# Bias tables read back by one skewed DMA in their final values and ordered by copies on GpSimd, in place of matmuls on TensorE

## The reference, cut to what matters

```python
def grouped_head_bias(bias_table, dist, ...):       # rel_bias (32, 20)
    return bias_table[rel_bucket(dist)]             # one value per distance and head
# heads 0-3: dense attention, 4-11: the compressed/selected/windowed branch, 12-19: window of 128 with sinks
s = q @ k.T * scale + grouped_head_bias(...)        # masked where dist < 0 (heads 12-19 also dist >= 128)
s_c = q @ k_cmp.T * scale + bias(qpos - cmp_end)    # cmp_end = 16 b + 31, b = 0..14
```

## Time and profile before

| what | us |
|---|---|
| median of 3 runs (3497.65 to 3503.95) | 3498.44 |
| the profiled execution | 3502.94 |
| its span | 3501.2 |
| TensorE busy | 3340.7 (95%) |
| VectorE busy | 1847.7 (53%) |
| ScalarE busy | 1565.8 (45%) |
| GpSimd busy | 143.6 (4%) |

### The profile page before, as it was taken

How to read it: one execution, slowest core, us unless ns; L and a number is a source line. 1 busy time by engine, 2 the same in 40 slices (tenths; PEclk the granted TensorE clock), 3 DMA queues, 4 the chain that set the end, 5 groups by cost and what they waited for, 6 DMA issues and landing times.

```text
span 3501.2 us, 39804 instructions
## 1 busy us (share of the span) xinstructions
PE 3340.7 (95%) x16471; PEld 2776.9 (79%) x16471; DVE 1847.7 (53%) x2387; ACT 1565.8 (45%) x1918; POOL 143.6 (4%) x253
## 2 busy tenths in 40 slices
PE   8999999949999989999999999999999999999998
PEld 6898888837888878878888878886788788867886
DVE  5455455555455455454465454654554645544545
ACT  4344344424444444443344343465544534565444
POOL 0000000002000000000000000012100000122000
PEclk9999999969999999999899999999999999999999
DMA  6545555513555545555456545642455455633553
GB/s 211 191 158 180 182 186 186 170 60 97 184 180 192 180 149 176 186 176 185 147 161 202 171 158 189 186 134 97 141 187 186 162 183 178 172 100 113 187 190 109
DMA packets 323905, 576.24 MB, mean 165 GB/s; under 512 B 45258, under 2 KB 130353, under 8 KB 323597
## 3 DMA queue, kind: packets, MB, share of 16 engines
q1 hardware_dynamic: 321196, 566.71, 49.9%
q0 software_dynamic: 2384, 6.63, 0.7%
q10 hardware_dynamic: 144, 0.35, 0.0%
HBM read 571.53 MB, written 1.08 MB: 164 GB/s over the span
## 4 chain that ended last, share of the span: by engine, by line
PE 90%; DVE 5%; ACT 3%; issue 1%; DMA 0%; DVEq 0%; SPq 0%; ACTq 0%
PE up L1668 20%; PE up L1670 19%; PE up L1669 19%; PE acc L1668 8%; PE acc L1670 8%; PE acc L1669 8%; DVE w_lo L944 2%; ACT w_hi L564 2%; PE up L1943 1%; PE acc L1838 1%; PE up L2160 1%; DVE xT_lo L1056 1%; PE acc L1765 0%; ACT xT_hi L629 0%; PE acc L1845 0%
## 5 line engine op out<-in xcount | busy, mean ns | idle before, releaser
L944 DVE TENSOR_TENSOR w_lo<-raw,w_hi 128x2048 fp32r<-128x2048 f32 x543 | 1244.4, 2292 | 1352.9 <-ACT w_hi L564 1350.2
L564 ACT ACTIVATE w_hi<-raw 128x2048 fp32r<-128x2048 f32 x543 | 1040.7, 1917 | 1470.6 <-PE up L1670 1094.9
L1668 PE MATMUL up<-w_hi,xT_hi 128*128 128x512 f32 (+1 forms) x2500 | 989.8, 396 | 54.9 <-DVE xT_lo L1056 27.1
L1669 PE MATMUL up<-w_lo,xT_hi 128*128 128x512 f32 (+1 forms) x2500 | 979.1, 392 | 0.0
L1670 PE MATMUL up<-w_hi,xT_lo 128*128 128x512 f32 (+1 forms) x2500 | 979.0, 392 | 0.0
L1668 PEld LDWEIGHTS up<-w_hi,xT_hi 128*128 128x128 f32 x2500 | 474.2, 190 | 166.5 <-issue 49.5
L1670 PEld LDWEIGHTS up<-w_hi,xT_lo 128*128 128x128 f32 x2500 | 474.0, 190 | 98.6
L1669 PEld LDWEIGHTS up<-w_lo,xT_hi 128*128 128x128 f32 x2500 | 474.6, 190 | 94.2
L1668 PE MATMUL acc<-w_hi,ff_hi 128*128 128x512 f32 x1216 | 480.4, 395 | 3.5 <-DVE ff_lo L1075 3.5
L1670 PE MATMUL acc<-w_hi,ff_lo 128*128 128x512 f32 x1216 | 474.0, 390 | 0.0
L1669 PE MATMUL acc<-w_lo,ff_hi 128*128 128x512 f32 x1216 | 473.4, 389 | 0.0
(11 more groups left out here) (282 smaller groups left out, 2355.0 us busy)
## 6 DMA issues: line engine op xcount, KB each, us to landing
raw<-in_ffn_down SPq DMA_DIRECT2D x88, 1024.0 KB, 4.8
raw<-in_ffn_gate SPq DMA_DIRECT2D x80, 1024.0 KB, 5.1
raw<-in_ffn_up SPq DMA_DIRECT2D x80, 1024.0 KB, 5.1
raw<-in_ffn_wi SPq DMA_DIRECT2D x80, 1024.0 KB, 5.2
raw<-in_ffn_wo SPq DMA_DIRECT2D x44, 1024.0 KB, 4.9
raw<-in_w_in SPq DMA_DIRECT2D x38, 1024.0 KB, 5.1
raw<-in_conv_w_in SPq DMA_DIRECT2D x24, 1024.0 KB, 5.2
raw<-in_w_branch SPq DMA_DIRECT2D x12, 1024.0 KB, 5.0
```

The source lines that it names most:

```text
L564: nc.scalar.activation(w_hi[n % RING][:], raw[n % RING][:], ACT.Copy).then_inc(hi_ready, 1)
L944: nc.vector.tensor_tensor(w_lo[n % RING][:], raw[n % RING][:], w_hi[n % RING][:].bitcast(F32), ALU.subtract).then_inc(lo_ready, 1)
L1668: pe.matmul(ps, lh, rh, start=start, stop=False)
L1669: pe.matmul(ps, lh, rl, start=False, stop=False)
```

## The change

The one-hot matmul now makes, in one go, 512 values per head in rising distance (the first matmul 12 heads by 512 columns, the second 8 heads by 384), scaled as they leave PSUM; they are stored once in DRAM as rows of 512 and read back by one skewed DMA as `V`, in which the query order is right and the key order is reversed. GpSimd writes TC by 22 copies of one column for 8 heads each (128 x 8) and T by ten copies of 128 x 512 that read backward. The 60 one-column-block instructions of line 2006 and the 20 reversing ones of line 2018 are gone. The three table steps move: each stands right behind a norm (8, 9 and 11) and so right ahead of a feed-forward step; `after` skips them, and they no longer add the residual or split a tile. PE has something to do in `tables 1` alone, into banks `up[2]` and `up[3]`, and the feed-forward step behind it waits with `held` for VectorE's copies out of these banks, between `first_pair` and the first tile that writes them. Two buffers of `conv` move in the arena.

```diff
-    at = plan.index(("norm", 9))
-    plan[at:at] = [("tables", 0)]
-    at = plan.index(("norm", 10))
-    plan[at:at] = [("tables", 1)]
-    plan += [("tables", 2)]
+    for part, row in enumerate((8, 9, 11)):
+        at = plan.index(("norm", row)) + 1
+        plan[at:at] = [("tables", part)]
...
-        U = carve(5376, 20, 256)
-        rv = carve(10496, 2, 384)
+        V = carve(5376, 20, 256)
+        rv_a, rv_c = arena[0:12, 10496:11008], arena[0:8, 13204:13716]
...
-            return next((s for s in plan[i + 1:] if s[0] != "norm"), ("end",))
+            return next((s for s in plan[i + 1:] if s[0] not in ("norm", "tables")), ("end",))
... ScalarE
             def tables(part):
-                arrive()
-                arrive()
-                settle()
                 if part != 1:
                     return
-                act.wait_ge(tab_dve, seen.next(tab_dve))
+                act.wait_ge(tab_dve, seen.next(tab_dve, 2))
                 nc.scalar.activation(ssh[:, 4:8], ssh[:, 0:4], ACT.Exp).then_inc(tab_act, 1)
... VectorE
             def tables(part):
-                residual()
-                settle()
                 if part == 0:
+                    nc.vector.memset(TC[:, :, 7:NCMP], NEG / HSCALE)
+                    nc.vector.memset(rv_c[:, 384:512], NEG / HSCALE)
                     nc.vector.memset(relb, NEG).then_inc(arena_free, 1)
                     return
                 if part == 2:
-                    flipped_tables()
+                    dve.wait_ge(tables_ready, seen.next(tables_ready, 2))
+                    dve.wait_ge(tab_act, seen.next(tab_act))
+                    ... (the four one-column steps on neglam, lines 1403 to 1406 before)
                     return
                 dve.wait_ge(tables_in, seen.next(tables_in, 16 * 8))
+                dve.wait_ge(tab_pe, seen.next(tab_pe))
+                nc.vector.tensor_scalar(rv_a, up[2][0:12, :], 1.0 / HSCALE, None, ALU.mult)
+                nc.vector.tensor_scalar(rv_c[:, 0:384], up[3][0:8, 0:384], 1.0 / HSCALE, None, ALU.mult).then_inc(rv_ready, 1)
+                nc.vector.tensor_copy(pos2[:].rearrange("p i v j -> p (i v j)"), up[3][:, 384:448]).then_inc(tab_dve, 1)
... (lines 1383 to 1390 follow as before; lines 1391 to 1413 go)
... TensorE
+                if held:                       # in ffn, between first_pair and the first up tile
+                    pe.wait_ge(tab_dve, seen.next(tab_dve))
...
             def tables(part):
-                ... (lines 1990 to 2021)
+                if part != 1:
+                    return
+                drain_banks()
+                pe.wait_ge(tables_in, seen.next(tables_in, 16 * 8))
+                pe.wait_ge(arena_free, 1)
+                pe.matmul(up[2][0:12, :], relb[:, 0:12], one_hots[:, 768:1280], start=True, stop=True)
+                pe.matmul(up[3][0:8, 0:384], relb[:, 12:20], one_hots[:, 768:1152], start=True, stop=True)
+                pe.transpose(up[3][:, 384:448], prows, ident[0:64, 0:64]).then_inc(tab_pe, 1)
... GpSimd
                 pool.wait_ge(rv_ready, 1)
+                pool.dma_start(scratch[0:12], rv_a).then_inc(rv_stored, 16)
+                pool.dma_start(scratch[12:20], rv_c).then_inc(rv_stored, 16)
                 pool.wait_ge(rv_stored, 32)
-                askew = bass.AP(scratch.tensor, 0, [[1, P], [384, 20], [1, 256]])
-                pool.dma_start(U, askew).then_inc(u_in, 16)
+                askew = bass.AP(scratch.tensor, 129, [[1, P], [512, 20], [1, 256]])
+                pool.dma_start(V, askew).then_inc(u_in, 16)
+                pool.wait_ge(u_in, 16)
+                for t, blocks in ((0, 7), (1, NCMP)):
+                    at = 96 + P * t
+                    for b in range(blocks):
+                        pool.tensor_scalar(TC[:, :, NCMP * t + b:NCMP * t + b + 1], V[:, 4:12, at - 16 * b:at - 16 * b + 1],
+                                           1.0, None, ALU.mult, ALU.bypass)
+                for g in range(10):
+                    last = pool.tensor_scalar(T[:, 2 * g:2 * g + 2, :], V[:, 2 * g:2 * g + 2, ::-1], 1.0, None, ALU.mult,
+                                              ALU.bypass)
+                last.then_inc(tables_ready, 2)
```

More of the change, by code:

```diff
@@ L163, in build @@
         g_rows = arena[0:G_ROWS, 0:D]
-        zconv = carve(0, 2, TOK + 2)
-        yconv = carve(520, 2, TOK)
+        zconv = carve(14000, 2, TOK + 2)
+        yconv = carve(14520, 2, TOK)
         Q = carve(0, NT, MH, QKH)
@@ L325, in build @@
         fin_ready = sem("fin_ready")
-        scratch = nc.dram_tensor("bias_rows", (20, 384), F32, kind="Internal").ap()
+        scratch = nc.dram_tensor("bias_rows", (20, 512), F32, kind="Internal").ap()
+        tables_ready = sem("tables_ready")
         vn_ready = sem("vn_ready")
@@ L1390, in tables @@
                 nc.vector.tensor_scalar(negsinks[:], sinks[:], -1.0, None, ALU.mult).then_inc(tab_dve, 1)
[L1391 to L1413, removed]
             def broadcast_rstd():
@@ L1931, in sg, with ffn @@
                 down(n, 3, False, True)
-            def ffn(s, n0, then):
+            def ffn(s, n0, then, held):
                 n = n0
@@ L1989, in tables @@
             def tables(part):
-                if part == 0:
+                if part != 1:
                     return
-                if part == 2:
-                    flipped_tables()
-                    return
+                drain_banks()
                 pe.wait_ge(tables_in, seen.next(tables_in, 16 * 8))
-                pe.wait_ge(tab_dve, seen.next(tab_dve))
-                pe.matmul(acc[0][0:12, 0:384], relb[:, 0:12], one_hots[:, 0:384], start=True, stop=True)
-                pe.matmul(acc[1][0:8, 0:384], relb[:, 12:20], one_hots[:, 384:768], start=True,
-                          stop=True)
-                pe.transpose(acc[2][:, 0:64], prows, ident[0:64, 0:64])
-                for t in range(NT):
-                    for b in range(NCMP):
-                        at = C_OHF - C_KEPT + 256 + P * t - 16 * b - 31
-                        i = NCMP * t + b
-                        last = pe.matmul(acc[3][:, 8 * i:8 * i + 8], one_hots[:, at:at + P], relb[:, 4:12], start=True,
-                                         stop=True)
-                last.then_inc(tab_pe, 1)
-                pe.wait_ge(tab_dve, seen.next(tab_dve))
-            def flipped_tables():
-                pe.wait_ge(u_in, seen.next(u_in, 16))
-                pe.wait_ge(x_ready, QUARTERS * (1 + residuals[0]))
-                for g in range(10):
-                    if g >= 4:
-                        pe.wait_ge(tab_dve, seen.next(tab_dve))
-                    pe.matmul(acc[g % 4][:], consts[:, C_FLIP:C_FLIP + P],
-                              U[:, 2 * g:2 * g + 2, :].rearrange("p h j -> p (h j)"), start=True,
-                              stop=True).then_inc(tab_pe, 1)
-                pe.wait_ge(tab_dve, seen.next(tab_dve, 4))
+                pe.wait_ge(arena_free, 1)
+                pe.matmul(up[2][0:12, :], relb[:, 0:12], one_hots[:, 768:1280], start=True, stop=True)
+                pe.matmul(up[3][0:8, 0:384], relb[:, 12:20], one_hots[:, 768:1152], start=True, stop=True)
+                pe.transpose(up[3][:, 384:448], prows, ident[0:64, 0:64]).then_inc(tab_pe, 1)
             def mix(s, n0):
@@ L2291, in _ @@
                     turned_x = after(i)[0] in XS
-                    ffn(s, n0, turned_x)
+                    ffn(s, n0, turned_x, plan[i - 1] == ("tables", 1))
                     residuals[0] += 1
@@ L2306, in _ @@
                     ple(s, n0)
-                if s[0] not in ("norm", "final"):
+                if s[0] not in ("norm", "tables", "final"):
                     turned_x = s[0] == "mix"
```

6 lines of the change are left out of this document (4 added, 2 removed).

## The result

The changed kernel takes 3455.3 us (median of 4 runs, 3452.32 to 3455.77), against 3499.03 for the kernel before (4 runs, 3497.65 to 3503.95): a ratio of 0.9874, 95% interval 0.9859 to 0.9888. The forecast was 3454.0 within 3447 to 3464. The profiled execution took 3455.64 (span 3453.8), 47.3 less than the one of before, where the sum said 44.5.

What follows compares the result with a forecast made beforehand. TensorE, busy for 95% of the span, was taken as the bound. Savings of 17.9 (norm 12), 22.35 (norm 10) and 4.3 (norm 9) sum to 44.5 us, which from the 3498.44 median gives 3454, range 3447 to 3464.

Steps and rivals of the forecast that it cites:

- Norm 12: Seam behind norm 12: with no table work left it becomes an undisturbed seam, 69.60 to 51.70, saving 17.9 us.
- Norm 10: Seam from norm 10 to `conv`: with no table work left it becomes that of norm 1, saving 22.35 us.
- The late transpose goes: Norm 9 seam: the transpose comes ahead of the last `down_half` again, worth 59.02 - 51.70 = 7.3 us.
- rival of late transposes: Early transpose stays late at norms 9 and 12, costing 7.3 us twice: 3469 us; chance 0.04.
- (a): Norm 9 seam: TensorE's new table matmuls, 1856 columns at the full clock, uncovered, take 1.75 us.
- (b): Norm 9: TensorE waits 0.8 us from S + 12.1 for VectorE's copies; S is the start of `first_pair`'s first product.
- (c): Norm 9: ScalarE's wait in `tables 1` delays the split of tile n0 + 3; TensorE waits 0.4 us, 0.5 with restart.
- The read back DMA: Behind norm 9, the read back runs beside weight loads; cost 0 to 0.1 us, taken as 0.
- the 3.0: Norm 9: new matmuls and waits together cost 3.0 us, bounds 1.6 to 8.5, leaving 4.3 of 7.3 saved.
- GpSimd's copies: 32 copies behind norm 9 take 23.5 us, ending 255 us before VectorE needs them behind norm 11; cost 0.
- GpSimd holds VectorE up: VectorE gets no turn until GpSimd's copies are done, TensorE loses 17.3 us: 3471 us; chance 0.05.
- The clock falls at norm 9: Two waits behind thin matmuls let TensorE's clock fall, up to 5.5 us more: 3459.5 us; chance 0.07.

Runs made afterwards that it cites:

- e1: Changed kernel with the first-half transposes put behind the last down projection again at the norm 9 and norm 12 seams; 3464.74 us.
- e2: Changed kernel's new table work, but with the three table steps at their old places, with their own residual, tile splitting and late transpose; 3474.94 us.
- e5: Changed kernel with GpSimd's read back of V held until the residual ahead of norm 10 is added; 3454.45 us.
- e8: The kernel before, unchanged, profiled a second time; 3494.72 us.
- e7: Changed kernel with the middle table step behind norm 11 instead of norm 9 and the last behind norm 12; 3455.02 us.
- e9: Changed kernel with table steps behind norms 8, 11, 12, VectorE's copies ahead of tile split and reciprocal norms, exponential in `tables 2`; 3449.85 us, ratio 0.9856.

## Why the prediction was right, point by point

- **Norm 12, 17.9 saved:** measured 17.9. **Norm 10, 22.35:** measured 22.3. The step that carried both, that a seam without table work becomes the undisturbed one, held to a tenth.
- **"The late transpose goes, which is worth 59.02 - 51.70 = 7.3":** the size was right for everything that leaves the seam, the name wrong. e1 prices the transpose at 3.45; about 3.9 was the table step's residual and tile split ahead of `xT_lo`, and e2 has 8.0 for it with the transpose. My rival of late transposes, 14.6 dearer, was overpriced by the same error: e1's two seams cost 3.9.
- **(a) own matmuls, 1.75:** 1.81, at the full clock, with no wait ahead of the first product.
- **(b) `held`, 0.8:** 1.13. TensorE came to it at S + 12.06 (12.1 worked out), the last copy ended at S + 13.14 and not 12.9: VectorE stood 0.22 ahead of the first copy, which I hadn't counted.
- **(c) `w_lo`, 0.4:** 0.24; tile n0 + 3 was ready at S + 19.1 for 18.9, but TensorE too was later by its first wait. Restarts cost 0.7 in all, where I had 0.2.
- **The step that failed is "The read back DMA": "0 to 0.1. I take 0".** It cost 1.22, with the restart 1.37 (e5). The ends of my range were for TensorE's own need for tile n0 + 6. I hadn't asked who else is behind that tile: the gate product stands on VectorE's queue behind the low part, and TensorE's transposes wait for the product, ahead of the tile.
- These make the norm 9 window 1.9 worse than forecast: 1.2 product, 0.3 `held`, 0.5 restarts, -0.2 `w_lo`, 0.1 own work. It stayed inside the bounds given, 1.6 to 8.5 for the 3.0, with 4.91.
- **GpSimd's copies, cost 0 with 255 us of cover:** held; the batch was 26.2 us for 23.5, since copies that meet a `w_lo` wait for its end. The rival "GpSimd holds VectorE up" had the direction the wrong way round. Small ones took 0.24 for 0.35, large ones 1.49 alone for 1.58.
- **"The clock falls at norm 9":** its window has 1.00.
- **The total** is nearer than its parts: 1.9 too much saved at norm 9, and 4.6 at a better clock outside the seams, which the sum put at nothing. Against the medians the gain is 3499.03 - 3455.3 = 43.7, and the seams make 42.7. So the forecast of the time was right by the seams. Of the 4.6, 2.1 in the second `mix` step is chance (e8); the 2.05 in the first goes with the change in every profile, and if it belongs to it, the sum lacked a term of 2 that the shortfall at norm 9 hid. That the forecast lies within 1.3 of the median is in part luck.

## What to carry to other kernels

Price a seam by the same seam where nothing disturbs it: the difference is right even where you name the wrong cause in it. When a large transfer is moved beside weight loads, don't stop at the matmul that needs the late tile; list what is queued behind each instruction that waits for it, on every engine. And put extra work where the engine already stands idle for a reason of its own: behind norm 9 it cost 4.9 us, behind norm 11, ahead of a gap of 2.05 us, 2.7, and none that can be seen once VectorE's copies and ScalarE's exponential were moved too.

## What the runs showed of the hardware

- A 2.6 MB read issued by GpSimd slowed 1 MB weight loads from about 5.1 to between 11.2 and 12.6 us to landing, and took 14.1 itself where it took 11.5 without them; the slowed loads cost TensorE 1.2 behind norm 9, 0.5 behind norm 11 in e7, and nothing there in e9.
- GpSimd's copies that read backward took 1.49 us for 128 x 512, and those in strides 0.24 for 128 x 8. Whether the direction costs anything isn't shown, as no copy of this form reads forward.
- Where `w_lo` (VectorE, two inputs) and a GpSimd copy met, GpSimd waited: 1.49 became up to 3.16 and 0.24 became 2.24, while 2.29 became at most 2.69.
- While GpSimd issued the 2.6 MB read, a short instruction of VectorE was held: 0.17 became 0.82 in e5, as 0.28 became 1.12 in the earlier trace rows.
- Two executions of one kernel differed in the granted clock at the same places, which moved single steps by 2 to 5 us (367.56 and 369.72, 209.70 and 214.65).
